# Attention inside a decoder block: Q copied into dilated order by GpSimd, one V buffer, and the normalise step in four parts

## The reference

```python
h = rms_norm(x, norm_mix_pre)
u_a, v_a, q, k, v_b, g_a, g_b = split(h @ w_in)
y_a = chunked_spatial_gating(gelu(u_a), gelu(v_a), ...)
# 16 heads of 64; three patterns: (window, dilation) = (128,1), (512,4), (2048,16)
# each: causal, 128 keys back in steps of the dilation, ALiBi bias
# outputs of the patterns weighted by their softmax denominators
y_b = dilated_attention_mixture(q / 8, k, v_b)
x = x + rms_norm((sigmoid(g_a + b0) * (y_a @ w_a) + sigmoid(g_b + b1) * (y_b @ w_b)) @ w_out)
x = x + rms_norm(square(relu(rms_norm(x) @ w_ff1)) @ w_ff2)
```

## Time and profile before

| | us |
|---|---|
| median of 2 runs | 1630.77 (1630.07 to 1631.47) |
| the profiled execution | 1634.41 |
| its span, slowest core (core 6) | 1632.8 |
| PE busy | 1338.0 (82%) |
| ACT busy | 747.5 (46%) |
| DVE busy | 665.5 (41%) |
| POOL busy | 119.6 (7%) |

### The profile page before, as it was taken

One profiled execution on the slowest core, in us unless ns is written; L12 is line 12 of the kernel. 1 busy time (PEld: TensorE's weight loads), 2 busy tenths in 40 slices (PEclk: granted clock), 3 DMA queues, 4 the chain that ended last, 5 costly groups with the idle time before them and its releaser, 6 DMA issues.

```text
span 1632.8 us, 22967 instructions; the slowest of 8 cores (1607.5 to 1632.8 us)
## 1 busy us (share of the span) xinstructions
PE 1338.0 (82%) x6971; PEld 694.5 (43%) x7092; DVE 665.5 (41%) x1136; ACT 747.5 (46%) x1351; POOL 119.6 (7%) x174
## 2 busy tenths in 40 slices
PE   1498928887888888867079999949999999999994
PEld 1243514554555545444034444424444444444442
DVE  2574771555556555556212232333303502511402
ACT  3323206767767677576135555433414413522401
POOL 1110011000101000000011111000000000000000
PEclk9999959998999999987589999969999999999997
DMA  8730036245656546424365344113344534534531
GB/s 206 128 33 1 1 49 104 57 95 94 104 95 115 93 101 122 92 67 111 70 76 60 34 39 39 74 56 118 141 169 132 189 129 160 201 131 166 194 129 77
DMA packets 115464, 165.45 MB, mean 101 GB/s; under 512 B 79232, under 2 KB 89856, under 8 KB 107136
## 3 DMA queue, kind: packets, MB, share of 16 engines
q0 software_dynamic: 96928, 104.87, 31.3%
q1 hardware_dynamic: 18416, 59.10, 11.8%
HBM read 174.31 MB, written 25.30 MB: 122 GB/s over the span
## 4 chain that ended last, share of the span: by engine, by line
PE 60%; DVE 13%; DMA 10%; ACT 8%; issue 7%; SPq 1%; DVEq 0%; ACTq 0%; POOLq 0%
PE pst L213 58%; DMA sb_denbc<-den_scr 6%; DMA sb_xt<-x 2%; DVE sb_acc L547 2%; ACT sb_acc L551 2%; ACT sb_Et L508 1%; DVE sb_bst L306 1%; DVE sb_big L309 1%; DVE sb_t L682 1%; ACT sb_acc L552 1%; DVE sb_acc L543 1%; DMA sb_wg<-w_in 1%; DVE sb_tmpm L339 1%; PE pst L729 1%; DVE sb_vaug L385 1%
## 5 line engine op out<-in xcount | busy, mean ns | idle before, releaser
L213 PE MATMUL pst<-sb_QZ,sb_KT 128*128 128x256 bf16 (+1 forms) x768 | 191.9, 360 | 53.3 <-ACT sb_Et L508 51.8
L213 PE MATMUL pst<-sb_h2T,sb_big 128*128 128x512 bf16 x1001 | 226.4, 382 | 3.6 <-ACT sb_h2T L720 1.3
L213 PE MATMUL pst<-sb_hT,sb_w2b 128*128 128x512 bf16 x1001 | 221.9, 379 | 4.0 <-DVE sb_hT L761 1.6
L508 ACT ACTIVATE sb_Et<-pst 128x512 bf16<-128x512 f32 x320 | 179.1, 575 | 84.8 <-PE pst L213 34.6
L213 PE MATMUL pst<-sb_hT,sb_wqkv 128*128 128x512 bf16 x730 | 192.7, 409 | 23.4 <-DVE sb_vaug L385 20.2
L213 PE MATMUL pst<-sb_hT,sb_wg 128*128 128x512 bf16 x501 | 116.5, 383 | 46.5 <-DMA sb_wg<-w_b 46.0
L213 PEld LDWEIGHTS pst<-sb_h2T,sb_big 128*128 128x128 bf16 x1024 | 100.6, 98 | 123.1 <-issue 7.3
L213 PEld LDWEIGHTS pst<-sb_hT,sb_w2b 128*128 128x128 bf16 x1024 | 99.6, 98 | 121.2 <-issue 3.4
L213 PE MATMUL pst<-sb_PT,sb_vaug 128*65 128x128 bf16 (+1 forms) x816 | 114.2, 266 | 38.3 <-DVE sb_PT L518 12.9
L761 DVE TENSOR_TENSOR sb_hT<-sb_hT 128x512 bf16<-128x512 bf16 x128 | 50.2, 422 | 225.1 <-ACT sb_hT L759 224.9
L518 DVE TENSOR_TENSOR sb_PT<-sb_Et,sb_EBh 128x512 bf16<-128x512 bf16 x176 | 73.0, 422 | 148.5 <-ACT sb_Et L508 145.6
(11 more groups left out here) (99 smaller groups left out, 1543.7 us busy)
## 6 DMA issues: line engine op xcount, KB each, us to landing
sb_big<-w_bf POOLq DMA_DIRECT2D x32, 1024.0 KB, 6.2
sb_w2b<-w_bf POOLq DMA_DIRECT2D x32, 1024.0 KB, 5.1
sb_stg<-w POOLq DMA_DIRECT2D x32, 512.0 KB, 6.0
w_bf<-sb_stg SPq DMA_DIRECT2D x32, 512.0 KB, 4.2
sb_xt<-x SPq DMA_DIRECT2D x16, 512.0 KB, 6.1
sb_denbc<-den_scr SPq DMA_DIRECT2D x32, 256.0 KB
sb_xo<-x SPq DMA_DIRECT2D x16, 512.0 KB, 4.2
out<-sb_xo SPq DMA_DIRECT2D x16, 512.0 KB, 2.8
```

The source lines that it names most:

```text
L213: S.op("pe", lambda e: e.matmul(out, lhsT=lhsT, rhs=rhs, start=start, stop=stop, skip_group_check=True), reads=reads, writes=writes, signa ...
L508: S.op("act", lambda e: e.activation(out=Et[es][:, 0:W], in_=ps[bank][:, 0:W], func=AF.Exp), reads=[], writes=[PK[bank], f"Et{es}"])
```

## The change

Q is copied once for each head into two more tiles, QP1 (stride 4 laid out contiguously) and QP2 (stride 16), by `tensor_copy` on POOL; the score matmuls of p = 1 and 2 then read contiguous slices of these. There is one set of QP tiles for all pairs. K is read as before. `vaug` has one buffer instead of two; the six transposing items of a pair move from the loop before into its own jobs 0 to 2. The other items of the next pair start at job 3: load at 3, V at 5 to 11, K at 13 to 19, Q at 21 to 27. The normalise step works on 512 columns instead of 1024, in four parts after 7, 9, 11 and 13 jobs.

```diff
-        vaug = [sb(ph, f"vaug{i}", [128, 48, 2, 65], BF16) for i in range(2)]
+        vaug1 = sb(ph, "vaug", [128, 48, 2, 65], BF16)
+        QP = [[sb(ph, f"QP{p}_{hh}", [128, SEQ], BF16) for hh in range(2)] for p in (1, 2)]
...
-        denbc = sb(ph, "denbc", [64, 1024], F32)
-        ytmp = sb(ph, "ytmp", [64, 1024], BF16)
+        denbc = sb(ph, "denbc", [64, 512], F32)
+        ytmp = sb(ph, "ytmp", [64, 512], BF16)
...
         def tokapN(T, p, kb, nblk):
-            if p == 0:
-                return T[:, 128 * kb:128 * kb + 128 * nblk]
-            if p == 1:
-                c, n = kb // 4, kb % 4
-                s = 512 * n + c
-                return T[:, s:s + 4 * (128 * nblk - 1) + 1:4]
-            return T[:, kb:SEQ:16]
+            return T[:, 128 * kb:128 * kb + 128 * nblk]
...
-            its = items[:5] + items[5:9] + [vtr(p, half) for p in range(3) for half in range(2)] + items[9:]
-            return its
+            return items, [vtr(p, half) for p in range(3) for half in range(2)]
...
+            for hh in range(2):
+                S.op("pool", lambda e, hh=hh, d=d: e.tensor_copy(
+                    out=QP[0][hh][:, :].rearrange("p (c j) -> p c j", c=4),
+                    in_=QZ[d][hh][:, :].rearrange("p (j c) -> p c j", c=4)), reads=[f"QZ{d}_{hh}"], writes=[f"QP1_{hh}"])
+                S.op("pool", lambda e, hh=hh, d=d: e.tensor_copy(
+                    out=QP[1][hh][:, :].rearrange("p (r i) -> p r i", r=16),
+                    in_=QZ[d][hh][:, :].rearrange("p (i r) -> p r i", r=16)), reads=[f"QZ{d}_{hh}"], writes=[f"QP2_{hh}"])
...
+                    qsrc, qk = (QZ[d][hh], f"QZ{d}_{hh}") if p == 0 else (QP[p - 1][hh], f"QP{p}_{hh}")
+                    mm(ps[bank][:, cw * i:cw * i + 128 * nblk], tokap(KT[d], slice(0, 128), p, kb), tokapN(qsrc, p, kb, nblk),
+                       i == 0, True, [f"KT{d}", qk], [PK[bank]], i == nk - 1)
...
-                            c0 = 1024 * hf
+                            c0 = 512 * hf
...
-                    deferred.append((gs[0] + 8, fin(0)))
-                    deferred.append((gs[0] + 12, fin(1)))
+                    deferred.append((gs[0] + 7, fin(0)))
+                    deferred.append((gs[0] + 9, fin(1)))
+                    deferred.append((gs[0] + 11, fin(2)))
+                    deferred.append((gs[0] + 13, fin(3)))
...
+                if si < 3:
+                    vtr_now[2 * si]()
+                    vtr_now[2 * si + 1]()
...
-                if si % 2 == 1 and ni < len(nxt):
+                if si % 2 == 1 and si >= 3 and ni < len(nxt):
```

More of the change, by code:

```diff
@@ L380, in build_nc @@
         accs = [sb(ph, f"acc{i}", [128, SEQ], F32) for i in range(2)]
-        denbc = sb(ph, "denbc", [64, 1024], F32)
-        ytmp = sb(ph, "ytmp", [64, 1024], BF16)
+        denbc = sb(ph, "denbc", [64, 512], F32)
+        ytmp = sb(ph, "ytmp", [64, 512], BF16)
         wqkv = [sb(ph, f"wqkv{i}", [128, 8, 384], BF16) for i in range(2)]
+        S.op("dve", lambda e: e.memset(vaug1[:].rearrange("p a b c -> p (a b c)"), 1.0), reads=[], writes=["vaug"])
         for i in range(2):
-            S.op("dve", lambda e, i=i: e.memset(vaug[i][:].rearrange("p a b c -> p (a b c)"), 1.0), reads=[], writes=[f"vaug{i}"])
             S.op("dve", lambda e, i=i: e.memset(QZ[i][0][64:128, :], 0.0), reads=[], writes=[f"QZ{i}_0"])
@@ L448, in f @@
                     S.op("act", lambda e: e.activation(
-                        out=vaug[d][:, b0:b0 + 8, :, 0:64], in_=pbf.rearrange("p (a h d) -> p a h d", a=8, h=2), func=AF.Copy),
-                        reads=[], writes=[PK[pk], f"vaug{d}"])
-                return f
-            its = items[:5] + items[5:9] + [vtr(p, half) for p in range(3) for half in range(2)] + items[9:]
-            return its
+                        out=vaug1[:, b0:b0 + 8, :, 0:64], in_=pbf.rearrange("p (a h d) -> p a h d", a=8, h=2), func=AF.Copy),
+                        reads=[], writes=[PK[pk], "vaug"])
+                return f
+            return items, [vtr(p, half) for p in range(3) for half in range(2)]
         deferred = []
@@ L460, in run_deferred @@
                 deferred.pop(0)[1]()
-        for it in prep_items(0):
+        its0, vtr_cur = prep_items(0)
+        for it in its0:
             it()
@@ L535, in emit_pv @@
                 for i, (sidx, ptcol, n, vblk, acol) in enumerate(pj["parts"]):
-                    mm(ps[bank][:65, acol:acol + n], vaug[d][:, 16 * p + vblk, hh, :], PT[sidx % NPT][:, ptcol:ptcol + n],
-                       i == 0, True, [f"vaug{d}", f"PT{sidx % NPT}"], [PK[bank]], i == np_ - 1)
+                    mm(ps[bank][:65, acol:acol + n], vaug1[:, 16 * p + vblk, hh, :], PT[sidx % NPT][:, ptcol:ptcol + n],
+                       i == 0, True, ["vaug", f"PT{sidx % NPT}"], [PK[bank]], i == np_ - 1)
                 if p == 0:
@@ L557, in f @@
                         def f():
-                            c0 = 1024 * hf
-                            S.dma("sp", lambda e: e.dma_start(out=denbc[:], in_=den_d[h:h + 1, c0:c0 + 1024].partition_broadcast(64)),
+                            c0 = 512 * hf
+                            S.dma("sp", lambda e: e.dma_start(out=denbc[:], in_=den_d[h:h + 1, c0:c0 + 512].partition_broadcast(64)),
                                   "den", reads=["dend", "denbc"], writes=["denbc"])
                             if hh == 0:
-                                S.op("dve", lambda e: e.tensor_tensor(out=ybT[0:64, hp, c0:c0 + 1024], in0=acc[0:64, c0:c0 + 1024],
+                                S.op("dve", lambda e: e.tensor_tensor(out=ybT[0:64, hp, c0:c0 + 512], in0=acc[0:64, c0:c0 + 512],
                                                                       in1=denbc[:], op=ALU.mult),
@@ L565, in f @@
                             else:
-                                S.op("dve", lambda e: e.tensor_tensor(out=ytmp[:], in0=acc[0:64, c0:c0 + 1024], in1=denbc[:], op=ALU.mult),
+                                S.op("dve", lambda e: e.tensor_tensor(out=ytmp[:], in0=acc[0:64, c0:c0 + 512], in1=denbc[:], op=ALU.mult),
                                      reads=[ak, "denbc"], writes=["ytmp"])
-                                S.dma("sp", lambda e: e.dma_start(out=ybT[64:128, hp, c0:c0 + 1024], in_=ytmp[:]), "ymv",
+                                S.dma("sp", lambda e: e.dma_start(out=ybT[64:128, hp, c0:c0 + 512], in_=ytmp[:]), "ymv",
                                       reads=["ytmp"], writes=[f"yb{hp}"])
```

8 lines of the change are left out of this document (5 added, 3 removed).

## The result

| | before | after |
|---|---|---|
| median, us | 1632.25 (10 runs) | 1815.76 (11 runs) |
| ratio to before | | 1.1102, 95% interval 1.1077 to 1.1127 |
| span of the slowest core, profiled | 1632.8 | 1814.5 |
| one middle attention loop | 67.7 | 89.5 |
| mean of loops 2 to 7 | 65.9 | 88.5 |

The change makes the kernel 11% slower, about 180 us. 1775 was forecast, with a range of 1685 to 1860: the sign and the size are right, the middle is 41 us low. The loop of 67.7 us that the forecast started from is the longest of those six (63.8 to 67.7).

What follows compares the result with a forecast made beforehand. PE was taken to lead, with ACT not far behind. Loops 2 to 7 at +18 us each (108), loop 1 +22 and loop 8 +14 made 144 on 1634.4: 1778, as median 1775; range 1685 to 1860.

Steps and rivals of the forecast that it cites:

- The permutation's worth: Dilated score matmuls: contiguous Q saves PE up to 5.6 (stride 16) plus 3.1 us (stride 4) a loop, stride-16 part mostly hidden.
- The floor of 0.46 by strided weights: Stride-16 score jobs: four strided K weight loads at 0.12 us could hold a job at 0.46, saving 3.7 instead of 5.6.
- The price of a copy: Pool's queue: each 128x2048 copy of Q takes 4.3 us, range down to 2.1.
- Late weights: QKV weights queued behind Pool's copies: PE waits some 5 us before each loop's first projection, 23 us in loop 1.
- the last copy ends at T + 0.8: Pool's last copy starts about T - 3.5 and takes 4.3 us; T is the loop's first score matmul.
- SP's queue: Denominator loads stand behind the FFN conversion's store: they leave at T + 20, first multiply T + 25.5 instead of T + 16.1.
- Four steps: Normalise on one denominator buffer: three gaps of 5.3 us, last multiply ends T + 42.1 instead of T + 27.1: +15 us.
- Jobs 20 to 27: Q projections now fall here: 15.2 us of ACT work, about 16 in all instead of 10.9: +5 us a loop.
- Jobs 28 to the end: Late loop: jobs 28 to 35 take 12.5 us against 12.6 before (0); tail 7.3 instead of 9.3 (-2).
- the collision: Rival: Pool copies keep DVE's two-SBUF-input products out while they run, +60 to +90 us, 1835 to 1865; chance 0.2.
- The whole stretch behind head 1's last multiply: Rest of the loop: jobs 13 to 19 at 0, 20 to 27 at +5, 28 to 35 at 0, tail -2 us.
- The faster rival: Strided Q is the bound and the rest hides: 8.7 us a loop saved, 1561 or 1575 us; chance 0.10.

Runs made afterwards that it cites:

- v_fin4: Kernel before with one vaug buffer, moved V items and four normalise parts on single buffers; strided Q, no copies: ratio 1.0684, +112 us.
- after_nocopy: Changed kernel without its 32 Pool copies, dilated score matmuls reading contiguous slices of Q itself (scores not the reference's): ratio 1.0569 to before, +93 us.
- fin4_only: Kernel before with only the normalise step changed, to four parts of 512 columns with one buffer: ratio 1.0373, +61 us.

## Why the prediction was right, point by point

**The permutation's worth.** Contiguous jobs at 0.22: right (0.21 and 0.24). 3.1 + 5.6 us a loop of which little arrives: right in the changed layout (79.9 us a loop in v_fin4, 77.9 in after_nocopy; 19 us in all), less so in that of before, where 5.2 us a loop arrive. The floor of 0.46 by strided weights does not show: four matmuls took 0.24.

**The price of a copy.** 4.3 us for all four: near for stride 16 (3.84 to 4.07 in twelve of sixteen, 5.4 in four), wrong for stride 4 (2.0), which is the lower bound.

**Late weights.** Right for loop 1: 17.3 us of wait, 23 forecast. Wrong for the others. The step that failed is "the last copy ends at T + 0.8": it ended at 439.82, T - 5.3 (T = 445.17). The copy began as forecast, right behind the last score matmuls, but T itself came later: 9.2 to 9.8 us behind these, against 4.0 in the kernel before and 5.8 to 7.1 in after_nocopy, DVE's products waiting for that very copy. PE came to job 5 at T + 14.3 rather than 12.5, and the weights were in by then.

**SP's queue.** The chain is the forecast one, 4 us early for the same reason: store at T + 14.7 (19.6 forecast), first multiply at T + 21.3 (25.5). On average over loops 2 to 7 the denominators leave at T + 16.1, 7.0 us later than before, where the forecast had 11; 4.3 of the 7.0 go with the queue's order.

**Four steps.** A gap of 5.3 forecast; measured 6.46, 4.40 and 5.70, mean 5.5. The last multiply ended at 483.75, T + 38.6, against T + 42.1 forecast. The mean of loops 2 to 7 is T + 37.9, and T + 24.9 before, where the forecast took 27.1 from the latest of the six. So the largest term of the sum, +15, measured +13.0, with two errors that cancel. Of the gap itself fin4_only shows 7.0 us a loop, more than the 3 to 6 that I expected of it alone.

**Jobs 20 to 27.** Job 28 came at 503.58, T + 58.4, where T + 66 was forecast. Job 20 was at 491.16, T + 46.0, so the stretch took 12.4 us: the +5 I put there is +1.5. ACT was busy 10.5 of the 15.2 us that I had put end to end; four of the eight Q evictions came only from 503.34 on, with jobs 28 and later.

**Jobs 28 to the end.** 12.5 and 7.3 us forecast, 503.58 to 521.41 = 17.8 and 521.41 to 534.67 = 13.3 measured. These 11 us a loop are the mis-sized terms, and most of the reason was among the rivals: the collision. I gave it 0.2 as an alternative to the forecast and priced it at +60 to +90; it came on top of the forecast's mechanism, at +44 to +58. The whole stretch behind head 1's last multiply, for which I had +3, is +9.5 in the change and +2.7 in after_nocopy, so without the copies the forecast of it holds.

The sum, in the two traces: loops 2 to 7 are 22.6 us longer each (18 forecast), loop 1 with the prologue 24.8 (22), loop 8 20.4 (14), 182 in all against 144. So 1775 was low because the collision was missing; 27 us of the shortfall lie in loops 2 to 7. That it is no further off is in part luck: late weights, SP's queue and jobs 20 to 27 were priced too high and make up for part of it. The faster rival had nothing for it: nothing in any run makes the changed order faster than before.

## What to carry to other kernels

Each part of a step that is cut up pays its own DRAM round trip unless the next one is already in flight: the split with two half buffers and early loads cost nothing, with one buffer it cost 61 us. GpSimd is not a free engine for copies beside a DVE that multiplies two SBUF operands, and a long instruction put on its queue delays every load behind it: put it after the loads, which gave 43 us back here, with the projections two jobs earlier; a place where DVE idles or works from PSUM would be the next thing to try, and was not run. Price a saving by the next engine in line: some 60 us less PE time over the eight loops were worth 25 to the slowest core.

## What the runs showed of the hardware

At the upper clock TensorE's moving operand in bf16 took 0.43 ns a column when contiguous (0.22 us for 512), 0.86 at stride 4 (0.44 us) and 1.8 at stride 16 (0.92 us); a strided stationary operand cost nothing visible (0.24 us for four matmuls of 128 columns with K at stride 16). The middle one was in the forecast against what the Trainium skill says of cachelines (SBUF — State Buffer, Door 1: The DMA port swizzle); the same jobs took 0.44 us at stride 4 in the kernel before and 0.21 contiguous in the changed one.

A Pool copy 128x2048 in bf16 takes 2.0 us reading at stride 4 and 3.84 at stride 16, a memset of the same size 1.80. The collision is whole: DVE's product ends 0.14 us after the copy's end (423.89 and 423.75) or 0.55 (440.37 and 439.82), though it was begun 0.26 and 0.29 us after the copy.

It goes the other way too. Four of the sixteen stride-16 copies took 5.4 to 5.5 us, and each of the four had been begun 0.05 to 0.14 us after a normalise multiply of DVE. One of them, with what DVE did:

```profile
525.73 0.68 DVE L569 TENSOR_TENSOR sb_big<-sb_acc,sb_denbc 64x512 bf16<-64x512 f32 x1 [1.16 <-DMA sb_denbc<-den_scr]
525.78 5.48 POOL L470 COPY sb_QP<-sb_QZ 128x2048 bf16<-128x2048 bf16 x1 [7.18 <-PE pst L213]
...
526.68 1.07 DVE L550 TENSOR_TENSOR sb_acc<-pst,sb_acc 65x512 f32<-65x512 f32 x1
527.66 4.21 DVE L519 TENSOR_TENSOR sb_PT<-sb_Et,sb_EBh 128x512 bf16<-128x512 bf16 x2
```

DVE's multiply, its next product (0.41 us) and its accumulate from PSUM keep their times and the copy is longer by 1.6 us; the product after these, begun 1.9 us into the copy, waits for the copy's end (the last row is that product and the next one).
